# A two-block transformer kernel: five stages between the experts of block 1 and the attention of block 2 become one stage that works token tile by token tile

## The reference, cut to what matters

```python
# end of first block: two rows of expert outputs per token, weighted, added to x; then its final norm
x = x + moe_ffn(...)                      # y = yb[dest] * sw; segment_sum: 2 rows per token
x = rms_norm(x, final_norm_g)
# second block
h = rms_norm_2(x, norm_mix_g)             # second norm over the same 1024 numbers per token
z = h @ w_in                              # columns 0:384 q latent, 384:640 kv latent, 640:672 rope key, ...
c_q = rms_norm_2(z[..., :384], q_norm_g)
c_kv = rms_norm_2(z[..., 384:640], kv_norm_g)
# then rope key and values from h and c_kv, and 8 heads of softmax attention
```

## Time and profile before

| | us |
|---|---|
| three runs | 5046.41, 5047.0, 5050.26 (median 5047.0) |
| profiled execution | 5049.6, of which the profiled span is 5047.7 |
| PE busy over the span | 4217.6 (84%) |
| DVE / ACT / POOL busy | 1370.1 / 993.0 / 387.7 |
| DMA over the span | 605.61 MB, mean 120 GB/s |
| combine, block 1 | starts at 2512.5 |
| norm2 | starts at 2555.9 |
| mp | starts at 2581.0 |
| mn | starts at 2662.7 |
| mv | starts at 2683.6, its first matmul at 2693.5 |
| first instruction of the heads' SP queue | 2725.7 |

### The profile page before, as it was taken

One profiled execution on the slowest core, in us unless ns is written; L12 is line 12 of the kernel. 1 busy time (PEld: TensorE's weight loads), 2 busy tenths in 40 slices (PEclk: granted clock), 3 DMA queues, 4 the chain that ended last, 5 costly groups with the idle time before them and its releaser, 6 DMA issues. The chain is left out here.

```text
span 5047.7 us, 89529 instructions
## 1 busy us (share of the span) xinstructions
PE 4217.6 (84%) x38565; PEld 2636.8 (52%) x38565; DVE 1370.1 (27%) x2272; ACT 993.0 (20%) x2287; POOL 387.7 (8%) x500
## 2 busy tenths in 40 slices
PE   7896788976999979999857987968769679997995
PEld 2343345864443457777643443448659564444664
DVE  2425111132000220101132552255564630003002
ACT  2200100021000121211123331023333310001333
POOL 0010000000000000000100000022322210000111
PEclk8898899987999989999978998989889889998998
DMA  5361111103111089999841002100000022102998
GB/s 208 137 182 67 68 42 58 34 0 112 44 29 48 29 300 368 366 372 365 290 163 24 7 2 74 37 1 3 3 2 4 2 90 52 44 33 76 371 379 316
DMA packets 355968, 605.61 MB, mean 120 GB/s; under 512 B 35112, under 2 KB 205511, under 8 KB 351784
## 3 DMA queue, kind: packets, MB, share of 16 engines
q1 hardware_dynamic: 318191, 454.91, 26.2%
q0 software_dynamic: 29168, 120.07, 6.9%
q10 hardware_dynamic: 8394, 27.46, 1.4%
HBM read 527.16 MB, written 75.24 MB: 119 GB/s over the span
## 5 line engine op out<-in xcount | busy, mean ns | idle before, releaser
L1629 PEld LDWEIGHTS experts_bank<-experts_uT,ex_wu 128*64 128x64 f32 x13312 | 557.5, 138 | 102.3 <-issue 102.3
L1629 PE MATMUL experts_bank<-experts_uT,ex_wu 128*64 128x96 f32 x13312 | 569.3, 248 | 46.3 <-PE experts_bank L1641 40.1
L1641 PE MATMUL experts_bank<-ex_wd,experts_hT 128*96 128x512 f32 x832 | 371.0, 595 | 0.0
L1806 PE MATMUL taps_bank<-rwkvh_hT,taps_w 128*128 128x512 f32 x480 | 211.7, 599 | 31.4 <-DMA taps_w<-in_w_in 25.4
L1275 DVE TENSOR_TENSOR merge_pr<-merge_bank,merge_sg 128x512 f32<-128x512 f32 x64 | 44.3, 691 | 711.5 <-ACT merge_sg L1262 437.9
L1690 DVE TENSOR_TENSOR experts_hT<-experts_si,experts_bank 128x384 f32<-128x384 f32 (+1 forms) x68 | 31.3, 460 | 733.6 <-PE experts_bank L1629 733.6
L1641 PEld LDWEIGHTS experts_bank<-ex_wd,experts_hT 128*96 128x96 f32 x832 | 130.2, 163 | 187.6 <-issue 185.3
L1248 PE MATMUL merge_bank<-mix_h2T,merge_w 128*128 128x512 f32 x512 | 222.3, 592 | 0.0
L1248 PE MATMUL merge_bank<-b2m_hT,merge_w 128*128 128x512 f32 x512 | 222.3, 592 | 0.0
L1806 PE MATMUL hin_bank<-mix_hT,hin_w 128*128 128x512 f32 x384 | 170.5, 603 | 14.7 <-DMA hin_w<-in_w_in 9.0
L1806 PEld LDWEIGHTS taps_bank<-rwkvh_hT,taps_w 128*128 128x128 f32 x480 | 90.6, 191 | 152.5 <-issue 146.2
(11 more groups left out here) (471 smaller groups left out, 6351.9 us busy)
## 6 DMA issues: line engine op xcount, KB each, us to landing
ex_wu<-in_expert_w SPq DMA_DIRECT2D x72, 2048.0 KB, 14.1
ex_wd<-in_expert_w SPq DMA_DIRECT2D x36, 2048.0 KB, 15.3
ex_wu<-in_w SPq DMA_DIRECT2D x64, 1024.0 KB, 11.1
ex_wd<-in_w SPq DMA_DIRECT2D x32, 1024.0 KB, 11.8
keep_rows<-experts_yo ACTq DMA_DIRECT2D x68, 384.0 KB, 5.9
keep_rows<-mix_hyT POOLq DMA_DIRECT2D x27, 768.0 KB, 4.7
mix_hT<-in_ada_w POOLq DMA_DIRECT2D x8, 2048.0 KB, 10.2
merge_w<-in_w_in SPq DMA_DIRECT2D x32, 512.0 KB, 5.2
```

The lines of the kernel that those rows point to most:

```text
L1629: last = pe.matmul(bk[2 + j][c:c + 64, h * BT:(h + 1) * BT], wu[:, s, j, k, h * P + c:h * P + c + 64], uT[:, s, k, :], start=(k == 0), sto ...
L1641: last = pe.matmul(bk[5 + j][0:BT, :], hT[:, k * BT:(k + 1) * BT], wd[:, s, k, j * HALF:(j + 1) * HALF], start=(k == 0), stop=(k == HT - 1))
L1806: last = pe.matmul(bk[s * 2 + h][:, :], wt[:, s, k, :], xT[:, k, h * HALF:(h + 1) * HALF], start=(k == 0), stop=(k == KT - 1))
```

## The change

The five phases combine (of block 1), norm2, mp, mn and the loading part of mv become one phase, `phase_entry`; mv keeps its arithmetic. X is not loaded back from DRAM. The weight of the latent projection (2.5 MB) is asked for by SP inside `phase_experts`, behind its last expert, into memory taken from the other end of SBUF; the operands of mv are asked for by SP at the start of `phase_entry`. The gather ring lies in the room of KTs and V, which are written later. hT is stored by token tile, in pieces of 512 bytes, by SP. The combine of block 2 stays as it was.

```diff
@@ phase_experts, SP, behind the last load
+            for dst, src, sem in ahead:
+                sp.dma_start(dst, src).then_inc(sem, 16)
-def phase_mla_norm(nc, name, K, zm, cT):
...
+def phase_entry(nc, I, K, T, rows, gain, x_dram, hT, hT_dram, w, wcame, cT, ring, ahead):
+    NT, G, X = SEQ // P, len(ring), K.X
+    parts = ((0, QL, 0, 3, "q_norm_g_2"), (QL, KVL, 3, 2, "kv_norm_g_2"))
...
+        tb, pj, cb = bk[0:2], (bk[2:4], bk[4:6]), bk[6:8]
+        steps = range(-3, NT + 2)
+        @b.gpsimd
+            for t in range(NT):
+                if t >= G:
+                    gp.wait_ge(added, t - G + 1)
+                for j in range(2):
+                    gp.indirect_dma_start(ring[t % G][:, j, :], None, rows, ...).then_inc(full[t % G], 16)
+        @b.sync
+            sp.dma_start(gr[:, :], gain...).then_inc(came, 16)
+            for dst, src, sem in ahead:
+                sp.dma_start(dst, src).then_inc(sem, 16)
+            for t in range(NT):
+                sp.wait_ge(normed, t + 1)
+                sp.dma_start(x_dram[tok(t), :], X[:, t, :]).then_inc(saved, 16)
+                for h in range(2):
+                    sp.wait_ge(evac[h], t + 1)
+                sp.dma_start(hT_dram[:, :, tok(t)], hT[:, :, tok(t)]).then_inc(kept, 16)
+        @b.tensor
+            def turn(t):       # waits yok t+1, evac[h] t; 8 transposes of ys -> tb; turned += 2
+            def project(t):    # waits wcame, znok t-1, evac[h] t+1; per part 8 matmuls -> pj; projected += 2
+            def latent(t):     # waits znok t+1, cout t; 5 transposes of zn -> cb; zturned += 1
+            for i in range(-1, NT + 1):
+                if i + 1 < NT:
+                    turn(i + 1)
+                if 0 <= i < NT:
+                    project(i)
+                if i >= 1:
+                    latent(i - 1)
+        @b.scalar              # for i in steps, each part for its tile u, where 0 <= u < NT
+            # u=i+1: wait turned 2u+1; 4 evacuations tb[0] -> hT; evac0
+            # u=i-1: per part: wait projected; Square of pj (accumulates), Sqrt; zrooted
+            # u=i-2: wait zturned; 5 evacuations cb -> cT; cout
+            # u=i+2: wait normed; Square of X, Sqrt; again
+            # u=i+3: wait added; Square of X, Sqrt; rooted
+        @b.vector              # the same
+            # u=i+1: wait turned 2u+2; 4 evacuations tb[1] -> hT; evac1
+            # u=i-1: wait zrooted; reciprocal; 2 multiplications pj -> zn; znok
+            # u=i+2: wait rooted; reciprocal; X = X * r * gain; normed
+            # u=i+3: wait full; X += w0 * row0; X += w1 * row1; added
+            # u=i+2: wait again; reciprocal; ys = X * r; yok
...
 def mla(nc, I, K, S, T, ahead, w_in, hT, oT):
-            phase_proj_N(nc, "mp", w_in[:, :, 0:LQ], KT, hT, 0, 8, 2, LQ // 2, ...)
-            phase_mla_norm(nc, "mn", K, zm, cT)
-        phase_mla_values(nc, "mv", I, w_in, rr("w_ukv_2"), hT, cT, rope, KTs, V)
+            phase_entry(nc, I, K, T, S.rows, I["final_norm_g"], S.x, hT, S.hT, ahead.wp, ahead.wpcame, cT,
+                        (four ring tiles in KTs and V), values_operands(...))
+            phase_mla_values(nc, "mv", wr, wv, fold, wcome, vcome, hT, cT, rope, KTs, V)
...
 def second(...):
-            phase_norm(nc, "norm2", K.X, 8, hT, ..., K, src=S.x)
...
```

More of the change, by code:

```diff
@@ L38, with __init__ @@
     spent = []
[L40 to L41 removed]
+    def __init__(self, nc, phase, side=None):
+        self.nc, self.phase, self.side, self.stack, self.own = nc, phase, side, ExitStack(), []
     def __enter__(self):
@@ L2317, in _ @@
[L2317 to L2321, removed]
-                        for k in range(kn):
-                            last = act.activation(cT[:, k0 + k, bass.ds(i * 256 + s * P, P)], bk[2 * s + j][:, k * P:(k + 1) * P],
-                                                  ACT.Copy, scale=vec(K.cols, gain, k))
-                        last.then_inc(evac, 1)
+            then = Chain(act, squared)
@@ new lines, in mean_root @@
+            def mean_root(src, out, n, root, sem):
+                then(act.activation(sq[:, 0:n], src, ACT.Square, accum_out=out))
+                act.activation(root, out, ACT.Sqrt, scale=1.0 / n, bias=K.eps[:, 0:1]).then_inc(sem, 1)
+            for i in steps:
+                if 0 <= i + 1 < NT:
+                    u = i + 1
+                    act.wait_ge(turned, 2 * u + 1)
+                    for k in range(4):
+                        last = act.activation(hT[:, k, tok(u)], tb[0][:, k * P:(k + 1) * P], ACT.Copy, scale=vec(K.cols, "norm_mix_g_2", k))
+                    last.then_inc(evac[0], 1)
+                if 0 <= i - 1 < NT:
+                    u = i - 1
+                    for j, (_, n, _, _, _) in enumerate(parts):
+                        act.wait_ge(projected, 2 * u + j + 1)
+                        mean_root(pj[u % 2][j][:, 0:n], sz[:, u, 0, j:j + 1], n, sz[:, u, 1, j:j + 1], zrooted)
+                if 0 <= i - 2 < NT:
+                    u = i - 2
+                    act.wait_ge(zturned, u + 1)
+                    for j, (_, _, k0, kn, name) in enumerate(parts):
+                        for k in range(kn):
+                            last = act.activation(cT[:, k0 + k, tok(u)], cb[j][:, k * P:(k + 1) * P], ACT.Copy, scale=vec(K.cols, name, k))
+                    last.then_inc(cout, 1)
+                if 0 <= i + 2 < NT:
+                    u = i + 2
+                    act.wait_ge(normed, u + 1)
+                    mean_root(X[:, u, :], ss[:, u, 3:4], D, ss[:, u, 4:5], again)
+                if 0 <= i + 3 < NT:
+                    u = i + 3
+                    act.wait_ge(added, u + 1)
+                    mean_root(X[:, u, :], ss[:, u, 0:1], D, ss[:, u, 1:2], rooted)
@@ L2327, in _ @@
+            act.wait_ge(zturned, NT)
         @b.vector
         def _(dve):
[L2329 to L2348, removed]
+            then = Chain(dve, chain)
@@ new lines, in _ @@
+            for i in steps:
+                if 0 <= i + 1 < NT:
+                    u = i + 1
+                    dve.wait_ge(turned, 2 * u + 2)
+                    for k in range(4, 8):
+                        last = dve.tensor_scalar(hT[:, k, tok(u)], tb[1][:, (k - 4) * P:(k - 3) * P], vec(K.cols, "norm_mix_g_2", k), None, ALU.mult)
+                    last.then_inc(evac[1], 1)
+                if 0 <= i - 1 < NT:
+                    u = i - 1
+                    dve.wait_ge(zrooted, 2 * u + 2)
+                    then(dve.reciprocal(sz[:, u, 2, :], sz[:, u, 1, :]))
+                    if u >= 2:
+                        dve.wait_ge(zturned, u - 1)
+                    for j, (c0, n, _, _, _) in enumerate(parts):
+                        last = dve.tensor_scalar(zn[:, u % 2, c0:c0 + n], pj[u % 2][j][:, 0:n], sz[:, u, 2, j:j + 1], None, ALU.mult)
+                    last.then_inc(znok, 1)
+                if 0 <= i + 2 < NT:
+                    u = i + 2
+                    if u == 0:
+                        dve.wait_ge(came, 16)
+                    dve.wait_ge(rooted, u + 1)
+                    then(dve.reciprocal(ss[:, u, 2:3], ss[:, u, 1:2]))
+                    dve.scalar_tensor_tensor(X[:, u, :], X[:, u, :], ss[:, u, 2:3], gr[:, :], ALU.mult, ALU.mult).then_inc(normed, 1)
+                if 0 <= i + 3 < NT:
+                    u = i + 3
+                    dve.wait_ge(full[u % G], 32 * (u // G + 1))
+                    then(dve.scalar_tensor_tensor(X[:, u, :], ring[u % G][:, 0, :], T.wt[:, 0, u:u + 1], X[:, u, :], ALU.mult, ALU.add))
+                    dve.scalar_tensor_tensor(X[:, u, :], ring[u % G][:, 1, :], T.wt[:, 1, u:u + 1], X[:, u, :], ALU.mult, ALU.add).then_inc(added, 1)
+                if 0 <= i + 2 < NT:
+                    u = i + 2
+                    dve.wait_ge(again, u + 1)
+                    then(dve.reciprocal(ss[:, u, 5:6], ss[:, u, 4:5]))
+                    if u >= 2:
+                        dve.wait_ge(turned, 2 * (u - 2) + 2)
+                    dve.tensor_scalar(ys[:, u % 2, :], X[:, u, :], ss[:, u, 5:6], None, ALU.mult).then_inc(yok, 1)
@@ L2689, in hyena, with moe @@
         phase_inverse(nc, I, K, prod, xc, hyT)
-def moe(nc, tag, I, K, S, hidden, scale, shift, names, gate, gain, out):
+def moe(nc, tag, I, K, S, T, hidden, scale, shift, names, gate=None, ahead=None):
     rgw, rgb, rew, reb, w1, w3, w2 = names
[L2696 to L2711, removed]
@@ new lines, in moe @@
+    ws = tuple(experts_to_tiles(I[w]) for w in (w1, w3, w2))
+    with Mem(nc, f"ex{tag}") as mx:
+        T.be = mx.sb("be", [1, MAXB], I32)
+        T.nb = mx.sb("nb", [1, 2], I32)
+        T.idx = mx.sb("idx", [BT, MAXB + 1], I32)
+        T.wu = mx.sb("wu", [P, 2, 2, KT, hidden])
+        T.wd = mx.sb("wd", [P, 2, hidden // P, D])
+        T.xg = mx.sb("xg", [BT, 2, D])
+        T.wufull = mx.sems("wufull0", "wufull1"); T.wdfull = mx.sems("wdfull0", "wdfull1"); T.xfull = mx.sems("xfull0", "xfull1")
```

(2 more changed lines are left out.)

193 lines of the change are left out of this document (113 added, 80 removed).

## The result

| | before | changed |
|---|---|---|
| median, us | 5046.7 (4 runs, 5045.58 to 5050.26) | 5004.14 (4 runs, 4998.02 to 5007.17) |
| ratio | | 0.9909, 95% interval 0.9897 to 0.9921 |
| profiled span | 5047.7 | 5004.1 |

The account below looks back on a forecast made before the run. Before, five stages ran one after the other, each bound differently; then PE at 10.1 us a step. 7.0 + 3.0 + 20.8 + 79.5 + 4.8 = 115.1 against 181.0; with mv's 1.6, 67.5 less: 4979.5 us, range 4971 to 4992.

Parts of the forecast that it names:

- Everything behind mv is as before: Stages after mv, block 2's experts included: no change in time.
- First add: Start of the new stage: 7.0 us as in combine plus 3.0 delay, so 10 us after the stage's start.
- The meeting with the operands: Mv's nine operand DMAs beside the first gather: delay 3.0 us by an equal share, bounds 0 and 7.9.
- Fill: New stage, adds, roots, gains, scaled rows and turns of the first tiles, one behind the other: 20.8 us.
- Middle: New stage, 8 projections 68.9, turns 5.6, latents 3.5 and low clock 1.5: sum 79.5 us.
- The loss at the low clock: PE starts the middle at the low clock: 1.5 us lost, bounds 0 and 1.9.
- Tail: After the last projection: square and root, DVE, five transposes, cT, hand-overs and phase end, 4.8 us.
- mv finds the high clock: Mv begins 2 us behind busy PE; its first 32 instructions take 13.8 instead of 15.44 us, 1.6 less.
- Rival A: New stage: DVE and ACT set the step, 11 to 12 us; costs 4.5 to 9.5, total 4984 to 4989; chance 0.12.
- B: New stage's start: first gather stands behind all operands, 4.9 us more than taken, total 4984; chance 0.05.
- C: New stage in lockstep: DVE's and PE's work follow each other, steps 18 to 19 us, total 5042; chance 0.03.
- D: TensorE stays at 1.2 GHz in the new stage: middle 78.0 us more, total 5057.5; chance 0.03.

Follow-up runs that it names:

- operands in mv: Changed kernel with 64 unused bytes ahead of block 2's expert weights, but mv asks for its own operands when it starts; 4995.39 us, ratio 0.989.
- 64-byte pad: Changed kernel with 64 unused bytes per partition ahead of block 2's expert weight buffers; 4978.03 us (0.9853), once more 4984.0 (0.9866).
- all aligned: Changed kernel with every tensor of 1 KB per partition or more on a multiple of 256 bytes, except the latent projection's weight; 4971.51 us, ratio 0.9844.
- kernel before with 192 bytes: Kernel before with 192 unused bytes per partition ahead of block 2's expert weights, starting them 192 past a multiple of 256; 5077.45 us, ratio 1.0051.
- changed kernel with 192 bytes: Changed kernel with 192 unused bytes per partition ahead of block 2's expert weights, starting them 128 past a multiple of 256; 5000.24 us, ratio 0.9902.
- split one: Changed kernel with 64 unused bytes ahead of block 2's expert weights and 128 more between ex_wu and ex_wd; 4984.92 us, ratio 0.9867.

## Why the prediction was wrong

The step that failed is one sentence, "Everything behind mv is as before": it put the stages behind mv at nothing without a reason, and block 2's experts took 25.8 us more, since the start of ex_wu had moved from a multiple of 256 bytes to 192 past one. The range had no room for it. The time forecast, 4979.5, is that of the changed kernel without the loss: with 64 bytes of padding 4978.03 and 4984.0, which is 70.8 and 68.3 us less than their pairs, where 67.5 were forecast. None of the rivals held it either. I named the stages behind mv only as something that would make the prediction wrong "if they move by themselves", and didn't look for how they could: the diff shows gate, modulation, X and the routing tables moved to the outermost allocation, and the page of the kernel before shows block 2's experts with a slice of 371 to 379 GB/s, the level of block 1's. In such a stage, with full DMA engines and a busy PE, a slower transfer has little room before it decides.

Step by step, forecast against the changed kernel's profile, us:

- First add 10.0 after the start; 9.05. The meeting with the operands was mis-sized: 3.0 forecast, some 1 us by the kernels without them, and up to 1 us more of the 2.0 has another cause that no run shows. The equal share that I took for the price is too much; the delay had the sign and the place that I gave it.
- Fill, from first add to the first projection: 20.8; 29.18 - 9.05 = 20.1.
- Middle 79.5; from the first projection's start to the last's end 108.63 - 29.18 = 79.45. The projection took 2586.98 - 2578.36 = 8.62 (forecast 8.6) and the step 10.04; splitting in 384 and 256 columns costs nothing. The loss at the low clock, 1.5 forecast, is 1.8: the first projection took 10.62 where the later ones take 8.78. Against that, turns and latents took 0.87 and 0.55 and not 0.9 and 0.6, so that the exact sum is in part two small errors that cancel. (In the prediction's sum 6 x 0.9 is 5.4 and 6 x 0.6 is 3.6; the total changes by 0.1.)
- Tail 4.8; 113.38 - 108.63 = 4.75.
- Together 115.1; 113.4.
- mv finds the high clock: 32 instructions in 13.8; 13.92, and 15.4 before. That it came out in the changed kernel was in part luck. Of the ten kernels with the new stage four have 13.92, five have 15.6, with mv as close behind busy PE (1.75 us) in each, and the one with the operands in mv 16.07. Those with 15.6 lost less in the first projection (9.2 to 9.5 us from its start to the next turn, for 10.5 to 10.7), so the forecast's total of 1.5 lost and 1.6 won holds in all of them to 1 us, and the division between the two does not.
- Rival A (DVE and ACT set the step): no wait of PE between steps, 0.77 us of slack. B: no, first add at 9. C: no, steps of 10.04. D: no, clock 1.00 in the running pipeline; the first projection rose to it, mean 0.82.
- That the weight asked for ahead costs nothing where it lies was right: experts of block 1 675.7 us in the changed kernel, 675.8 before. It is worth 2.4 us at the first add, which I hadn't counted for it.

What stays open: the opening stages (+5.3 us) and the stretch from the heads to block 2's experts (-5.1) moved by amounts that the other kernels also show among themselves (the stretch ran from 1927.6 to 1934.4). I take them for scatter of single profiles and have not shown more. Nor is it shown why the start of the destination slows rows of 1 KB and not those of 2 KB.

## What to carry to other kernels

When a change moves allocations, write down where each large DMA destination starts before and after, and check those that feed a stage with full DMA engines; here 64 bytes decided 26 us of 5000, in the stage with rows of 1 KB, and nothing in the one with 2 KB. When untouched code gets slower, compare the DMA rates of the same stage first. The rebuilt stage was forecast to 2 us out of 115 by adding up durations per engine and tile from rows and following the waits instruction by instruction. Ask ahead for what a later stage needs (10.2 us here); what is asked for beside the transfer that everything waits for costs something (about 1 us and 2.4 us here).

## What the runs showed of the hardware

- A stage that loads rows of 1 KB (two thirds of the weights' bytes) and of 4 KB from HBM to SBUF, 16 engines busy: 379 to 380 GB/s with the destinations on a multiple of 256 bytes (kernel before, 64-byte pad, all aligned), 349 to 352 with them 128 or 192 bytes past one (changed kernel, kernel before with 192 bytes, changed kernel with 192 bytes). Both offsets are multiples of 64, so that is not enough. With only the 4 KB rows beside the grid it was 379.
- Rows of 2 KB (block 1's experts, also with full DMA engines): SP's queue took 43.9 us of one engine per MB in the all-aligned kernel and 44.2 with the destination 192 bytes past a multiple of 256 (changed kernel), where the stage with rows of 1 KB has 44.8 and 48.7.
- An odd multiple of 256 did as well as a multiple of 512. ex_wu starts at 61184 = 239 x 256 in the all-aligned kernel and landed in 9.3 us, and at 60928 = 119 x 512 with the 64-byte pad, where it landed in 9.2; five kernels with the latter place have 9.2 to 10.4, and 11.1 in the split one, at the same rate in the steady window.
- The same code reached TensorE's full clock at different points: first projection 10.62 us and mv's first 32 matmuls 13.92 in one profile, 9.50 and 15.62 in another, with the same time to the heads to 0.2 us.
